# Strassen's seven block products for three quarters of a down projection, in turns with the up projection

## The reference, cut to what matters

```python
def sq_relu_mlp(h, w_up, w_down):
    return jnp.square(jax.nn.relu(h @ w_up)) @ w_down      # 2048 -> 8192 -> 2048

def second_block(x, ...):
    ...
        h = h + sq_relu_mlp(rms_norm_2(h, norm_ffn_g[i]), ffn_w_up[i], ffn_w_down[i])
    return rms_norm_2(h, final_norm_g)
```

## Time and profile before

| | us |
|---|---|
| median of three runs | 2039.89 |
| profiled execution, its own time | 2038.79 |
| its span | 2037.0 |
| TensorE matmuls busy | 1997.4 |
| VectorE busy | 1526.5 |
| ScalarE busy | 984.8 |
| GpSimd busy | 365.6 |

### The profile page before, as it was taken

One profiled execution on the slowest core, in us unless ns is written; L12 is line 12 of the kernel. 1 busy time (PEld: TensorE's weight loads), 2 busy tenths in 40 slices (PEclk: granted clock), 3 DMA queues, 4 the chain that ended last, 5 costly groups with the idle time before them and its releaser, 6 DMA issues.

```text
span 2037.0 us, 29904 instructions
## 1 busy us (share of the span) xinstructions
PE 1997.4 (98%) x11766; PEld 1735.0 (85%) x11766; DVE 1526.5 (75%) x2398; ACT 984.8 (48%) x1451; POOL 365.6 (18%) x276
## 2 busy tenths in 40 slices
PE   8999999999899999999999999999999999999997
PEld 7888888888788888888899978888888888888886
DVE  6877889887899986688899976776467557656754
ACT  6545454444444445557543446554344444434443
POOL 0000234333333410000287744000000000000000
PEclk9999999999999999999899999999999999999999
DMA  8655555445455555565456564555665666665553
GB/s 319 216 185 177 186 186 168 163 153 167 148 176 176 164 181 191 187 228 189 142 183 209 187 193 156 190 196 190 191 193 187 195 190 190 190 195 188 188 195 134
DMA packets 107132, 379.00 MB, mean 186 GB/s; under 512 B 12016, under 2 KB 15856, under 8 KB 106864
## 3 DMA queue, kind: packets, MB, share of 16 engines
q1 hardware_dynamic: 106992, 377.09, 57.6%
HBM read 374.06 MB, written 2.98 MB: 185 GB/s over the span
## 4 chain that ended last, share of the span: by engine, by line
PE 81%; DVE 13%; issue 3%; ACT 2%; DMA 1%; SPq 0%; DVEq 0%; ACTq 0%
PE bank L1854 34%; PE bank L1859 17%; PE bank L1845 7%; PE bank L1846 7%; PE bank L1847 7%; DVE wl L1042 3%; DVE bank L1607 3%; ACT wh L663 1%; PE bank L1868 1%; PE bank L1870 1%; PE bank L1869 1%; PE bank L1892 1%; DVE scr L1087 1%; PE bank L1993 1%; PE bank L1898 0%
## 5 line engine op out<-in xcount | busy, mean ns | idle before, releaser
L1042 DVE TENSOR_TENSOR wl<-raw,wh 128x1024 fp32r<-128x1024 f32 x610 | 760.6, 1251 | 370.8 <-ACT wh L663 368.8
L663 ACT ACTIVATE wh<-raw 128x1024 fp32r<-128x1024 f32 x680 | 712.4, 1055 | 543.3 <-PE bank L1847 226.8
L1854 PE MATMUL bank<-Hr,wh 128*128 128x512 f32 x2304 | 581.8, 394 | 1.3 <-ACT wh L663 0.9
L1854 PEld LDWEIGHTS bank<-Hr,wh 128*128 128x128 f32 x2304 | 415.1, 189 | 81.8 <-issue 5.9
L1854 PE MATMUL bank<-Yr,wh 128*128 128x512 f32 x1280 | 326.0, 397 | 15.4 <-ACT wh L663 8.5
L1859 PEld LDWEIGHTS bank<-Hr,wl 128*128 128x128 f32 x2304 | 314.2, 190 | 22.7
L1859 PE MATMUL bank<-Hr,wl 128*128 128x256 f32 x2304 | 321.1, 282 | 0.0
L1854 PEld LDWEIGHTS bank<-Yr,wh 128*128 128x128 f32 x1280 | 231.6, 190 | 60.4 <-ACT wh L663 8.5
L606 POOL TENSOR_TENSOR wl<-raw,wh 128x1024 fp32r<-128x1024 f32 x70 | 170.0, 2437 | 350.6 <-ACT wh L663 350.6
L1845 PE MATMUL bank<-wh,Yr 128*128 128x512 f32 x576 | 224.2, 389 | 0.0
L1846 PE MATMUL bank<-wl,Yr 128*128 128x512 f32 x576 | 224.1, 389 | 0.0
(11 more groups left out here) (334 smaller groups left out, 1925.3 us busy)
## 6 DMA issues: line engine op xcount, KB each, us to landing
raw<-in_w_up SPq DMA_DIRECT2D x128, 512.0 KB, 4.1
raw<-in_w_dn SPq DMA_DIRECT2D x128, 512.0 KB, 4.2
raw<-in_w_g SPq DMA_DIRECT2D x96, 512.0 KB, 3.5
raw<-in_w_p SPq DMA_DIRECT2D x80, 512.0 KB, 3.5
raw<-in_w_b SPq DMA_DIRECT2D x48, 512.0 KB, 3.4
raw<-in_w_out SPq DMA_DIRECT2D x32, 512.0 KB, 3.5
raw<-in_w_bx SPq DMA_DIRECT2D x16, 512.0 KB, 6.3
raw<-in_w_q SPq DMA_DIRECT2D x16, 512.0 KB, 4.1
```

Of the source, the lines that this page charges most:

```text
L663: e.activation(wh[:, c % WN, :], raw[:, c % RAW, :], ACT.Copy).then_inc(s_hi, 1)
L1042: e.tensor_tensor(wl[:, c % RAW, :], raw[:, c % RAW, :], wh[:, c % WN, :].bitcast(F32), ALU.subtract).then_inc(s_low_v, 1)
L1854: e.matmul(dst.rearrange("p (h t) -> p h t", h=2), wh[:, s, kk * 128:kk * 128 + 128], pair.both[:, :, k, :], start=first_part and kk == 0, ...
```

## The change

The first three quarters of the down projection (6144 of the 8192 hidden features) are computed by Strassen's scheme in Winograd's form. The 2x2 blocks are: two token halves by two neighbouring hidden slices on the left, two hidden slices by two output ranges of 512 on the right. Seven block products take the place of eight.

- The right factors: four blocks of weights are loaded (a, b, c, d) and three are made of them (v1, v2, v4); b is also overwritten by b + d. GpSimd makes these four sums per turn (`sums`), each of two 128x1024 tiles in SBUF. Each of the seven factors then gets its own high part (ScalarE) and low part (VectorE).
- The left factors: VectorE writes the squares of two up tiles as blocks of 128 columns (`squared_blocks`), makes three more by three subtractions and additions, and ScalarE and VectorE split all seven at once (896 columns) into `hidden`.
- The seven products (`product`) each take six matmuls of 128x512 and have a PSUM bank each; the up tiles share the eighth. A product is summed over four turns, and then VectorE spreads the seven banks over the four output blocks with 11 operations (`products_out`).
- The row scale of the norm is not applied to the hidden layer any more, but to the products when they are added to `xt` (a scale per token row, `r2`).
- The order: 11 up tiles alone, then 24 turns, each of four products (a, b, v1, d), one up tile, three products (v2, c, v4), one up tile; then five up tiles and four down groups of the old form.
- The rings have 12 raw buffers and 6 high buffers from the first turn on, in memory that is free by then, and VectorE and ScalarE work five chunks ahead in place of three. The load of `finB` moves behind the last up tile.

```diff
+PARTS = ("a", "b", "v1", "d", "v2", "c", "v4")
+QUADS, UP_ALONE, PAIRS = 24, 11, 10
...
+    for m in range(QUADS):
+        for half in (PARTS[0:4], PARTS[4:7]):
+            for part in half:
+                j = Job("dq", (m, part), "S", "w_dq", m, 1)
...
+            t = UP_ALONE + 2 * m + (half[0] != "a")
+            u = Job("up", t, "W", "w_up", t, 2)
...
+def ahead(c):
+
+    if c <= SW:
+        return range(c + 3, min(c + 4, NC))
+    return range(c + 3 if c == SW + 1 else c + 5, min(c + 6, NC))
...
-            if c == FFN + 8:
-                w.wait_ge(s_lnm, 1)
-                w.wait_ge(s_rstd, 5)
+            if c == end("up", 63) + 1:
+                w.wait_ge(s_mm, end("up", 63))
                 e.dma_start(finB, a["finB"]).then_inc(s_sg, 16)
...
+        def sums(m):
+
+            n = {p: unit_of(m, p) for p in PARTS}
+            b = {p: RAWS[RS[n[p]]] for p in PARTS}
+            raw_free(w, n["v1"])
+            landed(w, n["a"])
+            landed(w, n["b"])
+            e.tensor_tensor(b["v1"], b["a"], b["b"], ALU.add).then_inc(s_sum_w, 1)
+            landed(w, n["d"])
+            w.wait_ge(s_sum_w, 4 * m + 1)
+            e.tensor_tensor(b["b"], b["b"], b["d"], ALU.add).then_inc(s_sum_w, 1)
+            raw_free(w, n["v2"])
+            w.wait_ge(s_sum_w, 4 * m + 2)
+            e.tensor_tensor(b["v2"], b["v1"], b["d"], ALU.add).then_inc(s_sum_w, 1)
+            raw_free(w, n["v4"])
+            landed(w, n["c"])
+            w.wait_ge(s_sum_w, 4 * m + 3)
+            e.tensor_tensor(b["v4"], b["v2"], b["c"], ALU.add).then_inc(s_sum_w, 1)
...
             w.wait_ge(s_hi, HIGH[c])
-            e.tensor_tensor(wl[:, c % RAW, :], raw[:, c % RAW, :], wh[:, c % WN, :].bitcast(F32),
-                            ALU.subtract).then_inc(s_low_v, 1)
+            j = STEP[c][0]
+            if j.kind == "S":
+                w.wait_ge(s_sum_w, 4 * j.t[0] + {"a": 1, "b": 2, "v1": 3, "d": 3, "v2": 4, "c": 4, "v4": 4}[j.t[1]])
+            e.tensor_tensor(WLS[RS[c]], RAWS[RS[c]], WHS[HS[c]].bitcast(F32), ALU.subtract).then_inc(s_low_v, 1)
...
+        def squared_blocks(t, s):
...
+            to = blocks[:, 1:8:6, :] if t % 2 == 0 else blocks[:, 0:3:2, :]
+            e.scalar_tensor_tensor(to, s.rearrange("p (h t) -> p h t", h=2), 0.0,
+                                   s.rearrange("p (h t) -> p h t", h=2), ALU.max, ALU.mult).then_inc(s_sq, 1)
+            if t % 2 == 1:
+                w.wait_ge(s_sq, t + 1)
+                e.tensor_tensor(blocks[:, 3:5, :], blocks[:, 1:3, :], blocks[:, 7:8, :].broadcast_to((128, 2, 128)),
+                                ALU.subtract).then_inc(s_v, w.own())
+                w.wait_ge(s_v, w.n)
+                e.tensor_tensor(blocks[:, 5, :], blocks[:, 4, :], blocks[:, 1, :], ALU.add).then_inc(s_v, w.own())
+                w.wait_ge(s_v, w.n)
+                e.tensor_tensor(blocks[:, 6, :], blocks[:, 5, :], blocks[:, 0, :], ALU.subtract).then_inc(s_comb4, 1)
...
+        def products_out(g, part):
...
+            def add(x, p, r, done):
+                w.wait_ge(s_dq, n + done)
+                e.scalar_tensor_tensor(x, p, r, x, ALU.mult, ALU.add).then_inc(s_dq, 1)
...
+            if part == "a":
...
+                add(y[0][0], b["a"], r[0], 0)
+            elif part == "b":
+                add(y[1][0], b["b"], r[1], 0)
+                add(y[1][1], b["b"], minus[1], 0)
+            elif part == "d":
+                add(y[0][1], b["d"], minus[0], 0)
+            elif part == "v2":
+                e.tensor_tensor(zq, b["v2"], pq, ALU.subtract).then_inc(s_dq, 1)
+                add(y[1][0], zq, minus[1], 5)
+                e.tensor_tensor(pq, zq, b["v1"], ALU.subtract).then_inc(s_dq, 1)
+            elif part == "c":
+                add(y[0][0], b["c"], r[0], 1)
+            elif part == "v4":
+                add(y[1][0], b["v4"], r[1], 6)
+                add(y[0][1], pq, r[0], 7)
+                add(y[1][1], pq, r[1], 7)
...
+        def product(c, j):
+
+            m, part = j.t
+            g, d = divmod(m, 4)
+            dst = bank[PARTS.index(part)]
+            if d == 0 and g == 0:
+                w.wait_ge(s_comb, AT["up", UP_ALONE - 1].comb)
+                w.wait_ge(s_xt, 8)
+            elif d == 0:
+                w.wait_ge(s_pq, g)
+                w.wait_ge(s_dq, 11 * (g - 1) + FREED[part])
+            w.wait_ge(s_hidl, 8 * (m // 8) + 2 * d + 2)
+            w.wait_ge(s_hi, HIGH[c])
+            o = 128 * LEFT[part]
+            for i in range(2):
+                x = hidden[(8 * (m // 8) + 2 * d + i) % PAIRS]
+                rh = WHS[HS[c]][:, 512 * i:512 * i + 512]
+                e.matmul(dst, x[:, o:o + 128], rh, start=d == 0 and i == 0, stop=False)
+                e.matmul(dst, x[:, 896 + o:896 + o + 128], rh, start=False, stop=False)
+            low_there(c)
+            for i in range(2):
+                x = hidden[(8 * (m // 8) + 2 * d + i) % PAIRS]
+                ins = e.matmul(dst, x[:, o:o + 128], WLS[RS[c]][:, 512 * i:512 * i + 512], start=False,
+                               stop=d == 3 and i == 1)
+            ins.then_inc(s_mm, 1)
```

More of the change, by code:

```diff
@@ L184, with rings, unit_of @@
 P1, P1_END = first("p1g"), end("cv", 15)
+SW = AT["dq", (0, "a")].end - 1
+RAW2, WN2 = 12, 6
+def rings(n_old, n_new):
+    slot, before, last = {}, {}, {}
+    order = [(SW + i) % n_old for i in range(n_old)] + list(range(n_old, n_new))
+    for c in range(NC):
+        slot[c] = c % n_old if c < SW else order[(c - SW) % n_new]
+        before[c] = last.get(slot[c])
+        last[slot[c]] = c
+    return slot, before
+RS, RAW_BEFORE = rings(RAW, RAW2)
+HS, WH_BEFORE = rings(WN, WN2)
+LOADED = [c for c in range(NC) if STEP[c][1] is not None]
+LANDED, ASKED = {}, {}
+_n, _at = {}, 0
+for _c in LOADED:
+    LANDED[_c] = _n[RS[_c]] = _n.get(RS[_c], 0) + 1
+    if _c >= SW:
+        _at = max(_at, (RAW_BEFORE[_c] if RAW_BEFORE[_c] is not None else 0) + 1)
+        ASKED.setdefault(_at, []).append(_c)
+def unit_of(m, part):
+    return AT["dq", (m, part)].end - 1
+def ahead(c):
+    if c <= SW:
+        return range(c + 3, min(c + 4, NC))
+    return range(c + 3 if c == SW + 1 else c + 5, min(c + 6, NC))
+PAIR_LOW, PAIR_HIGH = {}, {}
+for _p in range(QUADS):
+    _e = AT["up", 2 * _p + 1].end
+    _l = min(_e + 3, AT["up", 2 * _p + 2].end)
+    PAIR_LOW[_l] = _p
+    PAIR_HIGH[max(_e + 1, _l - 1)] = _p
 def ended(c, stage):
@@ L430, in row @@
         return ap.rearrange("p (o t) -> p o t", o=1)
-    s_raw = [sem(f"s_raw{i}") for i in range(RAW)]
+    s_raw = [sem(f"s_raw{i}") for i in range(RAW2)]
     s_cst0, s_cst, s_bc, s_sg, s_out = sem("s_cst0"), sem("s_cst"), sem("s_bc"), sem("s_sg"), sem("s_out")
@@ L556, in sync @@
                 chunk(LN2 + 2)
-            if c + RAW - 1 < NC and c not in (LAST_PAD - 2, LAST_PAD - 1):
+            for n in ASKED.get(c, ()):
+                raw_free(w, n)
+                chunk(n)
+            if c + RAW - 1 < SW and c not in (LAST_PAD - 2, LAST_PAD - 1):
                 w.wait_ge(s_mm, c)
@@ L652, in gpsimd @@
                 tables((c - S5) // S5_STEP + 1)
+        for m in range(QUADS):
+            sums(m)
     def scalar(e):
@@ L954, in scalar @@
                     evac(j)
-            if 4 < c + 3 < NC and c + 3 not in HIGH_POST and c + 3 not in HIGH_LN and c not in (LN2 - 1, LN2):
-                high(c + 3)
+            for n in ahead(c):
+                if 4 < n and n not in HIGH_POST and n not in HIGH_LN and c not in (LN2 - 1, LN2):
+                    high(n)
+            if c in PAIR_HIGH:
+                pair_high(PAIR_HIGH[c])
             if c not in (end("gt", 1), LAST_PAD):
@@ L1692, in vector @@
         for c in range(1, NC + 1):
-            if c + 3 < NC and c not in (POST, LAST_PAD, LN2 - 1):
-                low(c + 3)
+            for n in ahead(c):
+                if c not in (POST, LAST_PAD, LN2 - 1):
+                    low(n)
+            if c in PAIR_LOW:
+                pair_low(PAIR_LOW[c])
             if c in (RX - 4, RX - 3):
@@ L1823, in chunk @@
                         w.wait_ge(s_comb, before.comb)
+                    elif before is not None and before.kind == "S":
+                        w.wait_ge(s_dq, QUADS // 4 * 11)
                     elif before is not None:
@@ L1828, in chunk @@
                 return
-            s, r = c % WN, c % RAW
+            if j.kind == "S":
+                product(c, j)
+                return
+            if j.stage == "up" and j.t == UP_ALONE:
+                w.wait_ge(s_eps, 5)
+            s, r = WHS[HS[c]], WLS[RS[c]]
             first_part, last_part = i == 0, i == j.nch - 1
@@ L1910, in stats @@
             return ins
-        def mean(src):
-            w.wait_ge(s_ones, 1)
-            e.matmul(bank[7][:, 0:T], ones, src, start=True, stop=True).then_inc(s_mean, 1)
         def mean_squares(n):
```

216 lines of the change are left out of this document (151 added, 65 removed).

## The result

The changed kernel takes 2166.99 us (median of four runs, 2166.28 to 2169.76), the kernel before, measured beside it, 2040.24 (median of four). The ratio is 1.0625, with a 95% interval of 1.0607 to 1.0644. The forecast was 2137 in a range of 2085 to 2190.

A forecast was written before the change was run, and what follows sets the result against it. The kernel was taken as bound by TensorE, and the changed one by VectorE and GpSimd sharing the way into SBUF: (26.3 - 22.06) x 24 = +102, - 8 + 3 = +97, giving 2137 us, range 2085 to 2190.

The forecast's parts named there:

- TensorE per turn: Seven products and four up chunks per turn take TensorE 20.70 us, against 22.06 before, saving 1.36 us.
- holds: VectorE operations with two SBUF inputs wait out a GpSimd sum: 2.2 us each, four per turn.
- VectorE per turn: VectorE's work in a turn, with 11 low parts where it had 8, sums to 18.3 us alone.
- GpSimd's price: One GpSimd sum of two 128x1024 SBUF tiles takes 2403 ns, four per turn 9.6 us.
- What the two do to each other: In the turns, VectorE and GpSimd instructions with two SBUF inputs exclude each other; the way into SBUF becomes the bound.
- upper bound of 27.1: Turn length in us, 18.3 + 8.8, if none of VectorE's work on PSUM tiles falls into holds.
- the 26.3 taken: Forecast turn length in us, 27.1 - 0.8, with a third of VectorE's PSUM work falling into holds.
- 8.8 less an overlap of 0.8: Per turn, 8.8 us of holds on VectorE, less 0.8 us of its PSUM work falling into them.
- The ends: Start of turns costs 3 us (0 to 6); first turn's sums beside lone up tiles save 8 (0 to 12).
- TensorE as the bound: Rival: GpSimd's sums fall into VectorE's waits in the turns, so TensorE sets the pace: 2009 us; 6 in 100.
- The clock: Rival: TensorE idles a fifth of each turn and its clock falls, some 40 us on top, 2177; 12 in 100.
- The signs named: Changed profile: TensorE some 93% busy, 80% in stage; low parts near 2 us; turns 26 us; products wait for low parts.

The follow-up runs named there:

- experiment 1: Changed kernel without GpSimd's four weight sums per turn; the three made factors are loaded as copies of block a instead: 2025.30 us, ratio 0.9931.
- experiment 5: Changed kernel with the four weight sums per turn made by VectorE between its low parts instead of by GpSimd: 2067.88 us, ratio 1.0137.
- experiment 2: Changed kernel with made factors loaded and GpSimd's four sums in place over only 512 columns: 2055.09 us, ratio 1.0082.

## Why the prediction was right, and where it was short

**TensorE per turn, 20.70 us.** Right: 21.02 at the mean in experiment 1, with all of it in place and no holds. Most turns there take 20.7, and the first of every four, when VectorE spreads the seven banks, about 21.9.

**VectorE per turn, 18.3 alone.** Slightly too high. From 1400 to 1920 us in experiment 5 VectorE was busy for 97.2%, so for 21.9 of the 22.54 us of a turn, where 22.8 was forecast; without its four sums (4.5 us) that is 17.4. That the turn came out at 22.54 is near the forecast because VectorE was also idle for 0.6 us of it. Starts 1.135 us apart are what the timeline there has again. By the sentence taken from the Trainium skill's page "VectorE: DVE Perf Modes", section "The DRAIN you can't avoid", that the next operation waits for an empty pipe, the turn would have been about 24 us (an estimate: 15 starts 0.09 us later each). The forecast left out how that section goes on: a next operation that is not held starts earlier. The trace agrees with that (1.13 to 1.14 us between starts of operations recorded at 1.22).

**GpSimd's price.** For a sum left alone 2392 to 2422 ns in the line shown; forecast 2403. The estimate from the Trainium skill's page "GPSIMD Engine Reference", section "Performance versus the Vector engine", half of its 4497 ns for 2048 columns or 2.25 us, is 6% short of these.

**What the two do to each other.** Right, and shown by doses: 21.0, 22.0 and 26.5 us a turn for none, half and whole. The 23 turns with sums beside them take 27.0 us at the mean, just under the upper bound of 27.1 and 0.7 above the 26.3 taken. Their parts come from the changed kernel's rows. The 238 low parts of the stretch have a mean of 1858 ns where experiment 1 has 1220, which is 152 us more in all, and the 37 squares 990 in place of 425, 21 us more. That makes 173 us beside 88 of GpSimd's sums, 2.0 us each, or 8.1 a turn: what 8.8 less an overlap of 0.8 had said. VectorE was busy for 555 of the 580 us, so for 25.9 of the 27.0; less the 8.1, its own work is 17.8, against 18.3. The term that was missing is 1.2 us a turn in which it was idle, 0.9 of them before low parts, for ScalarE's high part (7.1 + 5.4 + 3.1 + 3.0 us in 21.5 turns), which itself waits for a buffer that TensorE frees. I had taken VectorE to work without a gap once it was the bound. The two misses together are 0.7 us a turn, 17 us of the 30 missed.

**The ends.** Wrong, by the other 13. The forecast was -8 + 3 = -5. The 8 us credited for the first turn's sums were nearly there: three of the four ran beside the lone up tiles, the sums stay ahead to the end, and the last turn is 27.0 - 20.7 = 6.3 us shorter for it (this stands in the 26.77). But the waits are 8.9 + 3.9 + 1.7 = 14.5 where 3 were taken, so the ends come to +8. The step that failed is that the first turn's sums would run beside the lone up tiles at no cost: TensorE's wait before the first product is 3.8 us without the sums (experiment 1) and 8.9 with them, above the bound of 6. The changed kernel's timeline at the start of the turns:

```profile
1376.33 2.93 POOL L746 TENSOR_TENSOR raw<-raw 128x1024 f32<-128x1024 f32 x1 [3.34 <-DMA raw<-in_w_dq]
...
1379.30 1.06 ACT L795 ACTIVATE wh<-raw 128x1024 fp32r<-128x1024 f32 x1 [4.85 <-POOL raw L746]
1380.27 0.36 ACT L809 ACTIVATE upb<-bank 128x256 f32<-128x256 f32 x1
...
1381.54 0.41 DVE L1236 TENSOR_TENSOR upb<-upb,bank 128x256 f32<-128x256 f32 x1
1381.72 2.34 POOL L749 TENSOR_TENSOR raw<-raw 128x1024 f32<-128x1024 f32 x1 [2.45 <-PE bank L2085]
1381.99 2.35 DVE L1260 SCALAR_TENSOR_TENSOR blocks<-upb 128x256 f32<-128x256 f32 x1
...
1385.48 0.95 ACT L820 ACTIVATE hidden<-blocks 128x896 fp32r<-128x896 f32 x1 [3.90 <-DVE blocks L1269]
...
1387.76 0.37 ACT L809 ACTIVATE upb<-bank 128x256 f32<-128x256 f32 x1
...
1390.04 0.41 DVE L1236 TENSOR_TENSOR upb<-upb,bank 128x256 f32<-128x256 f32 x1
...
1390.50 0.80 PE L2116 MATMUL bank<-wh,hidden 128*128 128x512 f32 x1 [8.87 <-DVE upb L1236]
```

ScalarE's queue stands still for 4.85 us, because its next high part is of a factor that GpSimd has yet to add (L746). Behind it stands the copy of the last but one up tile's half (1380.27), which VectorE adds at 1381.54. The next sum (1381.72) then holds VectorE's square of that tile for 2.35 us. ScalarE waits for the blocks made from it and only then comes to the copy of the last up tile's half, at 1387.76. VectorE adds it at 1390.04, behind other work in its queue, and only then may TensorE start. I had counted one copy and one addition, and had not asked what stands queued in front of them. For the wait of 3.9 us behind the turns, and the 1.7 at the lower clock after it, I had no term at all.

**The rivals.** TensorE as the bound (6 in 100) would have needed a shorter hold even than the 1.2 us that I wrote: at 1.1 us the turn was already 1.0 us over TensorE's (experiment 2). The clock (12 in 100) did fall, again and again: 0.92 in the turns, forecast as possible with "some 40 us on top". It came at a lower price: what a late TensorE can cost while VectorE is the bound is VectorE's idle time, 1.2 us a turn or some 27 us in all, and how much of that is the clock's stays open. There is a sign that part of it is: 12 of the 25 us idle in the stretch are eight pauses of 1.1 to 1.6 us, each of which begins within 4 us after a stretch at the lower level has ended. One of them: the granted clock is 0.52 from 1562.3 to 1569.2 us, and VectorE is idle from 1573.0 to 1574.6, waiting for ScalarE's high part. No run separates the two. Keeping TensorE busy to hold the clock up was not tried: all eight PSUM banks are taken.

**The signs named.** TensorE's share of 93% (84% in the stage, where 80 was forecast), low parts with a mean near 2 us (1.86), GpSimd's sums at up to 3.4 us and turns of 26 to 27 us came as forecast. The waits before products for low parts did not: they are 4 us in all, and the big ones (92 us) stand before the up tiles, where TensorE needs the bank that an operation far back in VectorE's queue has to free.

## What to carry to other kernels

- Before giving GpSimd a share of elementwise work, look for operations with two SBUF inputs on both engines. Here their times added: a sum on GpSimd cost VectorE 2.0 us, the same sum on VectorE itself 1.14, though VectorE was the busier engine.
- A saving of matmuls counts only as far as the other engines' work for the same turn stays under TensorE's new, shorter pace. Count each engine by start-to-start distances, count operations that exclude each other as one engine's, and leave some time for waits: VectorE as the bound was still idle for 1.2 us of 27.0.
- At a change of stage, ask not only which operations TensorE waits for, but what stands ahead of them in their engines' queues.

## What the runs showed of the hardware that was not expected

- With two SBUF inputs on both, VectorE and GpSimd alternate by whole instructions: low parts of 1219 ns go up to 3432 to 3471, GpSimd's sums from 2.4 to as much as 3.4 us. With one input on GpSimd's side (128x1024 scalings of 2.8 to 3.8 us), VectorE's two-input operations were late by 0.9 us at most, and VectorE's low parts had a mean of 1.36 us. The Trainium skill's page "SBUF — State Buffer", section "Who interferes with whom", has it that an instruction of VectorE with two SBUF inputs and one of GpSimd that reads SBUF contend, and that the one issued second is blocked until the first is over. The sums agree (2.2 us of 2.4); the scalings, which read SBUF too, do not: 0.9 us of 2.8 to 3.8 for any one low part.
- The granted clock of TensorE was 0.92 on average over 580 us of the changed kernel in which it was busy for 84%, with waits of up to 6.4 us before up tiles. Over the same stretch it was 0.97 in experiment 5 (busy for 94%) and 1.00 in experiment 1 (98.5%). Within the turns it went between the two levels: 0.52 from 1562.3 to 1569.2 us, so mostly 1.2 GHz, a stretch that begins 2 us into a wait of TensorE of 5.70 us, and 0.99 from 1569.2 to 1593.
